# Decoder trunk on one core: the recurrence's gate products as 64-row products per head, with the input gates moved between partitions by DMA

## The chip, the cores and the metric

The kernel runs on one core of a Trainium2 chip, in one launch. The metric is the device time of one execution in microseconds (us). Engines are named as in the profile: PE (TensorE matmuls), PEld (its weight loads), DVE (VectorE), ACT (ScalarE), POOL (GpSimd) and SP (SyncE, which here only issues the weight DMAs).

## The reference

256 tokens of width 1024 go through two layers. Each has a token mixer, a channel mixer (dense in layer 0, top 2 of 8 experts in layer 1) and a gated embedding, all in f32. The change touches one part of the token mixer, the RG-LRU:

```python
ub = u.reshape(bsz, seq, 16, 64)                       # 16 heads of 64 channels
r      = sigmoid(einsum('bsnc,ncd->bsnd', ub, w_a) + b_a)
i_gate = sigmoid(einsum('bsnc,ncd->bsnd', ub, w_x) + b_x)
log_a = -8.0 * r * softplus(-lam)
a = exp(log_a)
b = sqrt(-expm1(2.0 * log_a)) * (i_gate * u)
h[s] = a[s] * h[s-1] + b[s]                            # scan over the tokens
y_a = h * gelu(rnn_gate)
```

Beside it stands a differential attention of 8 heads with rotary q and k: two 64-channel score products per head, two softmaxes, their difference times v. Both branches are projected, gated, added and projected again.

## The kernel before

**Tiling.** Activations lie transposed in SBUF, channels on the 128 partitions: a tile [128, 8, 256] holds 1024 channels (8 tile rows t) of 256 tokens, so that a tile row has two 64-channel heads, on partitions 0 to 63 and 64 to 127. Large weights come in chunks of 1 MB, in six raw slots. Each f32 weight w is split into two rounded parts, `whi` (ACT, helper `hi`, line 665) and `wlo` = w - whi (DVE, helper `lo`, line 1141), and a product takes three matmuls: whi by xhi, whi by xlo, wlo by xhi (line 1829). There are three slots for the split chunks.

**Steps.** The mixer is a loop over steps c = 0 to 35, written out on every engine in the same order: in step c PE multiplies chunk c (48 matmuls of 256 columns), then does the small products of that step. ACT and DVE in step c first split chunk c+3, ACT's halves waiting until PE has finished the halves of chunk c (`s_pe`), and then do their own work of step c. Nothing else orders the engines but semaphores; each engine's instructions run in the order in which they are written.

- Steps 0 to 3: DVE scales the chunk into `RIN` and convolves it to `U` (`convolve`, 8 instructions per step).
- Steps 2 to 5: PE multiplies two tile rows of `U` by the block-diagonal `BD` (`gate_products`, line 1984). Per tile row there are two f32 products of 128 rows: the one with `w_a` goes to the first half of a bank, the one with `w_x` to the second half. The matrix BD holds both heads of a tile row on its diagonal and zeros elsewhere. ACT makes `T2` = r, `IG` = i_gate, `TH` = tanh of a multiple of r, one instruction each (`gate_functions`, lines 786 to 790).
- Steps 4 to 11: ACT copies the q and k chunks to `QT`; POOL issues four DMAs per chunk that exchange 32-partition groups into `QW` (`exchange`, line 554); DVE rotates in steps 6 to 13 (`rotate`, three instructions).
- Step 6: DVE multiplies `IG` by `U` (line 1249), ahead of the split of chunk 9; ACT takes the square root of TH into `SQ`, which lies on `U`'s memory and therefore waits for that (line 832). Steps 7 and 8: ACT turns T2 into a = exp(...) (`decays`, line 797, four tile rows each). Steps 8 to 15: DVE makes one tile row of b per step (`recurrence_input`, lines 1258 and 1260). Steps 13 and 17: DVE scans four tile rows (`scan`, line 1266).
- Steps 14 to 25: the attention, one head per step on each engine. PE makes the `scores` of head c-14 (lines 1997 and 2000, products of 64 rows: the two halves of a head lie on partitions 0 to 63 and 64 to 127 and go to two banks), DVE masks and takes the maximum (line 1291 and 1294, result `AMX`), ACT takes the exponentials (lines 841 and 846), DVE the difference, PE turns it (line 2010), ACT copies it (`WT`, line 860), PE multiplies by v (line 2021). The first scores wait until all eight rotations are done.

`SPLAM`, needed by TH, comes from a chain of small DVE instructions in step 1 of layer 0 (`constants`).

## Time and profile before

| | |
|---|---|
| three runs, median (lowest to highest) | 1826.87 us (1825.75 to 1829.56) |
| the profiled execution: time, span | 1828.0 us, 1826.3 us |
| granted PE clock, mean | 0.994 |
| PE busy | 1784.4 us, 98% |
| PEld busy | 1563.4 us, 86% |
| DVE busy | 1490.7 us, 82% |
| ACT busy | 1307.7 us, 72% |
| POOL busy | 112.5 us, 6% |
| DMA | 517.04 MB, mean 283 GB/s |

The profiled execution is one, and lies 1.1 us above the median. Busy times are unions over the span. An f32 product appears as two matmul records. The mixer of layer 0 lies at about 20 to 227 us, that of layer 1 at about 546 to 750 us.

### The profile page before, as it was taken

The page shows a single profiled execution, that of the slowest core. Times are in us where ns is not written, and L with a number is a line of the kernel's source. Part 1 is how long each engine was busy: PE and PEld are TensorE (multiplying, and loading weights), DVE is VectorE, ACT ScalarE, POOL GpSimd, SP SyncE. Part 2 cuts the span into 40 slices and gives each one's busy share as a digit, 9 for nine tenths or more (in the row PEclk, how much of TensorE's full clock was granted, in tenths as well). Part 3 has the DMA queues.
Part 4 walks back from the last instruction along what each step waited for, and adds up shares of the span by engine and source line. Part 5 has one row for each costly group of instructions (what it writes and reads, how often), then busy time and mean ns, then how long its engine had stood idle before and what let it go on. Part 6 is the DMA issues. An engine that isn't in the chain of part 4 may idle for free.

```text
span 1826.3 us, 29866 instructions
## 1 busy us (share of the span) xinstructions
PE 1784.4 (98%) x10569; PEld 1563.4 (86%) x10569; DVE 1490.7 (82%) x1958; ACT 1307.7 (72%) x1732; POOL 112.5 (6%) x138
## 2 busy tenths in 40 slices
PE   6999999999999999999999999999999999999997
PEld 6998999999889999978888888888888888888786
DVE  7888667666478886769989989989899898998997
ACT  6756547454477657467888888788888887888787
POOL 1200000000010200012000000010000100000300
PEclk8999999999999999999999999999999999999999
DMA  9663555566556744667999999999999999999992
GB/s 307 206 191 117 174 200 191 185 198 205 188 158 193 221 141 139 208 185 258 395 382 379 387 363 392 374 369 389 365 383 374 374 389 372 375 384 363 391 363 95
DMA packets 276050, 517.04 MB, mean 283 GB/s; under 512 B 10754, under 2 KB 114052, under 8 KB 275972
## 3 DMA queue, kind: packets, MB, share of 16 engines
q1 hardware_dynamic: 268400, 493.81, 76.4%
q0 software_dynamic: 7248, 22.06, 3.7%
q8 instruction: 50, 0.82, 0.2%
q14 instruction: 28, 0.23, 0.0%
q10 hardware_dynamic: 324, 0.12, 0.0%
HBM read 503.87 MB, written 7.88 MB: 280 GB/s over the span
## 4 chain that ended last, share of the span: by engine, by line
PE 78%; DVE 9%; ACT 8%; issue 2%; DMA 2%; ACTq 0%; DVEq 0%; SPq 0%
PE bank L1829 74%; DVE wlo L1141 4%; ACT whi L665 2%; DMA raw<-in_moe_w_up_dram 1%; PE bank L2299 1%; ACT SC L846 1%; ACT SQJ L676 1%; PE bank L1984 1%; DVE RIN L1266 1%; DVE SC L1294 1%; ACT L1052 0%; ACT L665 0%; ACT SC L841 0%; ACT L772 0%; ACT HH L728 0%
## 5 line engine op out<-in xcount | busy, mean ns | idle before, releaser
L1141 DVE TENSOR_TENSOR wlo<-raw,whi 128x1024 fp32r<-128x1024 f32 x880 | 1031.0, 1222 | 164.3 <-ACT whi L665 161.6
L665 ACT ACTIVATE whi<-raw 128x1024 fp32r<-128x1024 f32 x880 | 917.1, 1059 | 306.3 <-PE bank L1829 288.2
L1829 PE MATMUL bank<-HH,whi 128*128 128x256 f32 x1296 | 364.1, 281 | 0.0
L1829 PE MATMUL bank<-whi,XGH 128*128 128x512 f32 x896 | 355.8, 397 | 5.7 <-DVE wlo L1141 5.6
L1829 PE MATMUL bank<-HL,whi 128*128 128x256 f32 x1296 | 360.1, 278 | 0.0
L1829 PE MATMUL bank<-HH,wlo 128*128 128x256 f32 x1296 | 360.1, 278 | 0.0
L1829 PE MATMUL bank<-whi,XGL 128*128 128x512 f32 x896 | 350.5, 391 | 0.0
L1829 PE MATMUL bank<-wlo,XGH 128*128 128x512 f32 x896 | 349.4, 390 | 0.0
L1829 PEld LDWEIGHTS bank<-HH,wlo 128*128 128x128 f32 x1296 | 244.5, 189 | 0.0
L1829 PEld LDWEIGHTS bank<-HH,whi 128*128 128x128 f32 x1296 | 243.6, 188 | 0.9 <-issue 0.7
L1829 PEld LDWEIGHTS bank<-HL,whi 128*128 128x128 f32 x1296 | 243.8, 188 | 0.2
L1829 PEld LDWEIGHTS bank<-whi,XGH 128*128 128x128 f32 x896 | 168.6, 188 | 44.8 <-DVE wlo L1141 10.9
L1829 PEld LDWEIGHTS bank<-whi,XGL 128*128 128x128 f32 x896 | 168.4, 188 | 36.5
L1829 PEld LDWEIGHTS bank<-wlo,XGH 128*128 128x128 f32 x896 | 168.7, 188 | 33.2
L1829 PE MATMUL bank<-whi,ATH 128*128 128x512 f32 x448 | 176.8, 395 | 0.0
L1829 PE MATMUL bank<-whi,ATL 128*128 128x512 f32 x448 | 175.0, 391 | 0.0
L1829 PE MATMUL bank<-wlo,ATH 128*128 128x512 f32 x448 | 174.4, 389 | 0.0
L1829 PEld LDWEIGHTS bank<-whi,ATL 128*128 128x128 f32 x448 | 84.1, 188 | 18.1
L1829 PEld LDWEIGHTS bank<-wlo,ATH 128*128 128x128 f32 x448 | 84.2, 188 | 16.9
L1829 PEld LDWEIGHTS bank<-whi,ATH 128*128 128x128 f32 x448 | 84.1, 188 | 16.8
L1526 DVE TENSOR_TENSOR wlo<-raw,whi 128x1024 fp32r<-128x1024 f32 x56 | 67.2, 1223 | 31.1 <-ACT whi L951 29.9
L951 ACT ACTIVATE whi<-raw 128x1024 fp32r<-128x1024 f32 x56 | 58.8, 1059 | 42.1 <-PE bank L1829 41.4
(359 smaller groups left out, 2098.9 us busy)
## 6 DMA issues: line engine op xcount, KB each, us to landing
raw<-in_moe_w_gate_dram SPq DMA_DIRECT2D x112, 1024.0 KB, 8.0
raw<-in_moe_w_up_dram SPq DMA_DIRECT2D x112, 1024.0 KB, 8.6
raw<-in_moe_w_down_dram SPq DMA_DIRECT2D x112, 1024.0 KB, 7.2
raw<-in_w_in_dram SPq DMA_DIRECT2D x56, 1024.0 KB, 6.0
raw<-in_ffn_w_gate_dram SPq DMA_DIRECT2D x14, 1024.0 KB, 5.1
raw<-in_ffn_w_up_dram SPq DMA_DIRECT2D x14, 1024.0 KB, 5.1
raw<-in_ffn_w_down_dram SPq DMA_DIRECT2D x14, 1024.0 KB, 5.0
raw<-in_w_proj_a_dram SPq DMA_DIRECT2D x8, 1024.0 KB, 5.1
```

The source lines that it names most:

```text
L665: nc.scalar.activation(whi[b % SPL][:, r], raw[b % RAW][:, r], ACT.Copy).then_inc(s_hi, 1)
L676: nc.scalar.activation(SQJ[:, 0:src.shape[-1]], src, ACT.Square, accum_out=sums).then_inc(s, 1)
L846: ins = nc.scalar.activation(r, r, ACT.Exp, bias=AMX[:, q, 2 + m:3 + m], scale=HD ** -0.5, accum_out=ASUM[:, q, 2 + m:3 + m])
L951: nc.scalar.activation(whi[nb % SPL][:, r], raw[nb % RAW][:, r], ACT.Copy).then_inc(s_hi, 1)
L1141: v.tensor_tensor(wlo[b % SPL][:, r], raw[b % RAW][:, r], whi[b % SPL][:, r].bitcast(F32), ALU.subtract).then_inc(s_lo, 1)
L1266: ins = v.tensor_tensor_scan(RIN[:, i, 3:], T2[:, i, :], IG[:, i, :], 0.0, ALU.mult, ALU.add)
L1294: ins = v.tensor_tensor_reduce(SC[:, q, SEQ * (m + 1):SEQ * (m + 2)], B[4 + m][:, P:P + SEQ], MASK[:, :], 1.0, -3e38, ALU.add, ALU.max, AM ...
L1526: v.tensor_tensor(wlo[nb % SPL][:, r], raw[nb % RAW][:, r], whi[nb % SPL][:, r].bitcast(F32), ALU.subtract).then_inc(s_lo, 1)
L1829: ins = mm(dst, a, b, start=start and n == 0, stop=stop and n == 2, skip_group_check=True)
L1984: ins = mm(bank[:, SEQ * kind:SEQ * kind + SEQ], BD[:, kind, t, :], U[:, t, :], start=True, stop=True)
L2299: ins = nc.tensor.transpose(B[6][:, P * i:P * i + P], MA[:, f % 2, P * i:P * i + P], IDENT[:, :])
```

## The change

`BD` becomes one matrix per tile row. Its rows 0 to 63 hold, side by side, w_a and w_x of the lower head, its rows 64 to 127 w_x and w_a of the upper head, and no zeros are left. Each tile row still has two f32 products, but each now uses 64 rows: the lower head's result (r on partitions 0 to 63, i on 64 to 127) goes to one bank and then to `T2`, the upper head's (i on 0 to 63, r on 64 to 127) to another bank and then to `IG`. Since i comes out on the other head's partitions, POOL moves it: per pair of tile rows two DMAs of 64 partitions write `IX`, which lies on `V`'s memory. TH and the decays read r from two tiles and so take two instructions of 64 partitions each. `SQ` now lies on `K` (in place of TH) instead of on `U`. DVE multiplies IX by U in step 8 instead of step 6, and makes two tile rows of b per step in steps 8 to 11 instead of one per step in steps 8 to 15. New waits: the decays and the multiplication on the DMAs (`s_ix`), the copy of V in step 12 and the rotations of k on b (`s_bl`), the second product on a bank's earlier reader (`s_tc`, layer 0). The bias rows b_a and b_x are loaded twice each in halves, so that they fit the partitions; b_x by two DMAs of POOL ahead of its first memsets. POOL's two memsets of BD are gone.

```diff
-        BD = at("BD", o_bd, [P, 2, KT, P])
+        BD = at("BD", o_bd, [P, KT, P])
-        SQ = at("SQ", o_gel, [P, KT, SEQ])
+        IX = at("IX", o_q + 16 * KB, [P, KT, SEQ])
-        OALL, TH = Q, K
+        OALL, TH, SQ = Q, K, K
+        LRU_BANK = ((3, 7), (5, 6))
...
@@ gpsimd
+            v = lru_bx.rearrange("l (t p) -> (l t) p", p=P)
+            for h in range(2):
+                pool.dma_start(R2[96 + 16 * h:112 + 16 * h, HD - HD * h:P - HD * h],
+                               v[:, HD * h:HD * h + HD]).then_inc(s_ldp, 16)
...
-            pool.memset(BD[:, :, :, :], 0.0).then_inc(s_bdz, 1)
...
-                        pool.dma_start(BD[HD * h:HD * h + HD, kind, :, HD * h:HD * h + HD], pairs[h]).then_inc(s_bd, 16)
+                        d = HD * (kind ^ h)
+                        pool.dma_start(BD[HD * h:HD * h + HD, :, d:d + HD], pairs[h]).then_inc(s_bd, 16)
...
+            def input_halves(layer, j):
+                pool.wait_ge(s_gx, 4 * layer + j + 1)
+                two = slice(2 * j, 2 * j + 2)
+                pool.dma_start(IX[0:HD, two, :], T2[HD:P, two, :]).then_inc(s_ix, 16)
+                pool.dma_start(IX[HD:P, two, :], IG[0:HD, two, :]).then_inc(s_ix, 16)
...
             def exchange(layer):
+                input_halves(layer, 0)
+                input_halves(layer, 1)
                 for i in range(8):
                     n = 8 * layer + i
+                    if i in (1, 2):
+                        input_halves(layer, i + 1)
                     pool.wait_ge(s_eva, eva(layer, 4 + i))
...
@@ scalar
-                    bank = B[3 if t % 2 == 0 else 7]
                     col = layer * KT + t
-                    link(nc.scalar.activation(T2[:, t, :], bank[:, 0:SEQ], ACT.Sigmoid, bias=V2[:, 80 + col:81 + col]))
-                    nc.scalar.activation(IG[:, t, :], bank[:, SEQ:], ACT.Sigmoid, bias=V2[:, 96 + col:97 + col])
+                    for h, dst in enumerate((T2, IG)):
+                        c = 96 + 16 * h + col
+                        ins = nc.scalar.activation(dst[:, t, :], B[LRU_BANK[t % 2][h]][:, 0:SEQ], ACT.Sigmoid,
+                                                   bias=V2[:, c:c + 1])
+                    link(ins)
+                    if t % 2:
+                        act.sem_inc(s_gx, 1)
...
-                    nc.scalar.activation(TH[:, t, :], T2[:, t, :], ACT.Tanh,
-                                         scale=SPLAM[:, col:col + 1]).then_inc(s_ga, 1)
+                    for h, src in enumerate((T2, IG)):
+                        r = slice(HD * h, HD * h + HD)
+                        ins = nc.scalar.activation(TH[r, t, :], src[r, t, :], ACT.Tanh, scale=SPLAM[r, col:col + 1])
+                    ins.then_inc(s_ga, 1)
...
             def decays(layer, g):
+                act.wait_ge(s_ix, 128 * (layer + 1))
...
-                    ins = nc.scalar.activation(T2[:, t, :], T2[:, t, :], ACT.Exp, scale=SPNEG[:, col:col + 1])
+                    for h, src in enumerate((T2, IG)):
+                        r = slice(HD * h, HD * h + HD)
+                        ins = nc.scalar.activation(T2[r, t, :], src[r, t, :], ACT.Exp, scale=SPNEG[r, col:col + 1])
...
                         if c == 12:
                             act.wait_ge(s_rc, 6 * layer + 2)
+                            act.wait_ge(s_bl, KT * layer + KT)
...
                     if c == 6:
                         act.wait_ge(s_ga, KT * (layer + 1))
-                        act.wait_ge(s_iu, layer + 1)
...
@@ vector
             def input_gates(layer):
-                dve.wait_ge(s_ga, KT * (layer + 1))
-                v.tensor_tensor(IG[:, :, :], IG[:, :, :], U[:, :, :], ALU.mult).then_inc(s_iu, 1)
+                dve.wait_ge(s_ix, 128 * (layer + 1))
+                v.tensor_tensor(IX[:, :, :], IX[:, :, :], U[:, :, :], ALU.mult).then_inc(s_iu, 1)
...
                 dve.wait_ge(s_qs[i % 4], 64 * (2 * layer + i // 4 + 1))
+                if i >= 4:
+                    dve.wait_ge(s_bl, KT * layer + 2 * i - 6)
...
-                    if c == 6:
-                        input_gates(layer)
...
-                    if 8 <= c < 16:
-                        recurrence_input(layer, c - 8)
+                    if c == 8:
+                        input_gates(layer)
+                    if 8 <= c < 12:
+                        recurrence_input(layer, 2 * c - 16)
+                        recurrence_input(layer, 2 * c - 15)
...
@@ tensor
+                if n == 1:
+                    pe.wait_ge(s_tc, 4)
-                for kind in range(2):
-                    ins = mm(bank[:, SEQ * kind:SEQ * kind + SEQ], BD[:, kind, t, :], U[:, t, :],
-                             start=True, stop=True)
+                for h in range(2):
+                    r = slice(HD * h, HD * h + HD)
+                    ins = mm(B[LRU_BANK[t % 2][h]][:, 0:SEQ], BD[r, t, :], U[r, t, :], start=True, stop=True)
```

DVE, steps 7 (its last two rows here) and 8, before:

```order
L1282 TENSOR_TENSOR Q<-QT,COSR 128x512
L1283 TENSOR_TENSOR Q<-Q,QW 128x512 [waits s_dc]
L1141 TENSOR_TENSOR wlo_60<-raw_54,whi_57 128x1024 [waits s_hi] x2
L1281 TENSOR_TENSOR QW<-QW,SINR 128x512 [waits s_qs2]
L1282 TENSOR_TENSOR Q<-QT,COSR 128x512
L1283 TENSOR_TENSOR Q<-Q,QW 128x512 [waits s_dc]
L1258 SCALAR_TENSOR_TENSOR SQ<-T_96,SQ 128x256 [waits s_al,s_iu,s_sq]
L1260 TENSOR_TENSOR IG<-IG,SQ 128x256 [waits s_dc]
```

and step 8 with the head of step 9 now (`K` is the memory that SQ lies on):

```order
L1169 TENSOR_TENSOR wlo_60<-raw_54,whi_57 128x1024 [waits s_hi] x2
L1311 TENSOR_TENSOR QW<-QW,SINR 128x512 [waits s_qs2]
L1312 TENSOR_TENSOR Q<-QT,COSR 128x512
L1313 TENSOR_TENSOR Q<-Q,QW 128x512 [waits s_dc]
L1277 TENSOR_TENSOR IX<-IX,U 128x2048 [waits s_ix]
L1286 SCALAR_TENSOR_TENSOR K<-T_96,K 128x256 [waits s_al,s_iu,s_sq]
L1288 TENSOR_TENSOR IG<-IX,K 128x256 [waits s_dc]
L1286 SCALAR_TENSOR_TENSOR K<-T_96,K 128x256
L1288 TENSOR_TENSOR IG<-IX,K 128x256 [waits s_dc]
L1169 TENSOR_TENSOR wlo_58<-raw_49,whi_55 128x1024 [waits s_hi] x2
```

The multiplication of 2048 elements per partition has moved behind the rotation of step 8, and a second tile row of b stands behind it, ahead of the split of step 9.

ACT, steps 7 and 8 before (L797 are the decays, L665 the split of chunk 11):

```order
L797 ACT_TABLE_LOAD
L797 ACTIVATE T_96<-T_96,SM 128x256 x4
L665 ACTIVATE whi_57<-raw_54 128x1024 [waits s_pe,s_w5]
L665 ACTIVATE whi_57<-raw_54 128x1024 [waits s_pe]
L812 ACTIVATE QT<-bank 128x512 [waits s_qr]
L797 ACTIVATE T_96<-T_96,SM 128x256 x4
```

and step 7's now:

```order
L825 ACT_TABLE_LOAD
L825 ACTIVATE T_96<-T_96,SM 64x256 [waits s_ix]
L825 ACTIVATE T_96<-IG,SM 64x256
L825 ACTIVATE T_96<-T_96,SM 64x256
L825 ACTIVATE T_96<-IG,SM 64x256
L825 ACTIVATE T_96<-T_96,SM 64x256
L825 ACTIVATE T_96<-IG,SM 64x256
L825 ACTIVATE T_96<-T_96,SM 64x256
L825 ACTIVATE T_96<-IG,SM 64x256
L684 ACTIVATE whi_57<-raw_54 128x1024 [waits s_pe,s_w5]
```

Four instructions of 128 partitions have become eight of 64, ahead of the split for which DVE's step 8 waits.

POOL, the exchanges of steps 5 and 6 now (before, the QW rows stood alone, one after another):

```order
L554 DMA IX<-T_96 64x512 [waits s_gx]
L555 DMA IX<-IG 64x512
L572 DMA QW<-QT 32x512 [waits s_u,s_eva]
L572 DMA QW<-QT 32x512 x3
L554 DMA IX<-T_96 64x512 [waits s_gx]
L555 DMA IX<-IG 64x512
L572 DMA QW<-QT 32x512 [waits s_u,s_eva]
L572 DMA QW<-QT 32x512 x3
```

The last two IX DMAs stand between the second and the third exchange.

## Rows read from the trace of the kernel before

**Rows 1.** The page, part 1: busy us, share of the span, instructions.
```profile
PE 1784.4 (98%) x10569; PEld 1563.4 (86%) x10569; DVE 1490.7 (82%) x1958; ACT 1307.7 (72%) x1732; POOL 112.5 (6%) x138
```

**Rows 2.** Chain of waits, layer 0, 63 to 119 us: start, length, what.
```profile
63.37 45.24 PE bank L1829 x384
108.63 1.07 ACT whi L665
...
113.59 2.44 DVE RIN L1266 x4
116.05 2.36 DVE wlo L1141 x2
```

**Rows 3.** The same chain in layer 1.
```profile
563.51 1.99 PE bank L1984 x8
...
587.47 45.24 PE bank L1829 x384
...
640.15 2.36 DVE wlo L1141 x2
```

**Rows 4.** Timeline of PE, attention: start, length, line, operands, [idle before, releaser].
```profile
177.44 0.52 PE L2010 MATMUL bank<-IDENT,SC 128*128 128x128 f32 x3 [1.05 <-ACT WT L860]
...
701.54 0.52 PE L2010 MATMUL bank<-IDENT,SC 128*128 128x128 f32 x3 [1.05 <-ACT WT L860]
```

**Rows 5.** Timeline of PE, layer 0, the gate products of step 2.
```profile
38.99 1.89 PE L1984 MATMUL bank<-U,BD 128*128 128x256 f32 x8
40.52 0.47 PE L1829 MATMUL bank<-HH,whi 128*128 128x256 f32 x1
40.83 0.28 PE L1829 MATMUL bank<-HL,whi 128*128 128x256 f32 x1
```

**Rows 6.** Timeline of PE, layer 0, the first scores, products of 64 rows.
```profile
113.97 0.28 PE L1829 MATMUL bank<-whi,HL 128*128 128x256 f32 x1
114.17 0.49 PE L1997 MATMUL bank<-K,Q 64*128 64x128 f32 x4
114.50 0.60 PE L2000 MATMUL bank<-K,Q 64*128 64x256 f32 x4
115.03 0.39 PE L1829 MATMUL bank<-whi,HH 128*128 128x256 f32 x1
115.25 0.28 PE L1829 MATMUL bank<-wlo,HH 128*128 128x256 f32 x1
```

**Rows 7.** Chain of waits, layer 0, step 3.
```profile
45.83 0.51 ACT K L790
...
47.66 1.13 PE bank L1984 x4
```

**Rows 8.** Timeline of ACT, layer 0, steps 7 and 8.
```profile
77.57 1.71 ACT L797 ACTIVATE T<-T,SM 128x256 f32<-128x256 f32 x4
79.19 2.24 ACT L665 ACTIVATE whi<-raw 128x1024 fp32r<-128x1024 f32 x2
```

**Rows 9.** Timeline of DVE, layer 0, steps 6, 8 and 9.
```profile
65.78 2.29 DVE L1249 TENSOR_TENSOR IG<-IG,U 128x2048 f32<-128x2048 f32 x1 [1.64 <-ACT K L790]
...
80.26 2.42 DVE L1141 TENSOR_TENSOR wlo<-raw,whi 128x1024 fp32r<-128x1024 f32 x2 [1.16 <-ACT whi L665]
82.60 0.68 DVE L1281 TENSOR_TENSOR QW<-QW,SINR 128x512 f32<-128x512 f32 x1
...
84.53 0.42 DVE L1258 SCALAR_TENSOR_TENSOR SQ<-T,SQ 128x256 f32<-128x256 f32 x1
...
85.33 1.22 DVE L1141 TENSOR_TENSOR wlo<-raw,whi 128x1024 fp32r<-128x1024 f32 x1
87.11 1.22 DVE L1141 TENSOR_TENSOR wlo<-raw,whi 128x1024 fp32r<-128x1024 f32 x1 [0.57 <-ACT whi L665]
```

**Rows 10.** POOL's timeline, one exchange; DMA issues, KB each and us to landing.
```profile
63.51 1.96 POOL L554 DMA_DIRECT2D QW<-QT  x4 [2.04 <-ACT QT L812]
...
QW<-QT POOLq DMA_DIRECT2D x64, 64.0 KB, 4.5
```

More of the change, by code:

```diff
@@ L281, in bass_hybrid_rglru_diffattn_moe @@
         s_iu = sem("s_iu")
+        s_gx = sem("s_gx")
+        s_ix = sem("s_ix")
         s_bl = sem("s_bl")
@@ L1229, in convolve @@
                 if j == 0:
-                    dve.wait_ge(s_bdz if layer else s_pool, 3 if layer else 12)
+                    dve.wait_ge(s_bdz if layer else s_pool, 1 if layer else 12)
                 for tap in range(4):
@@ L1981, in gate_products @@
                     pe.wait_ge(s_ga, n - 1)
-                bank = B[3 if t % 2 == 0 else 7]
-                for kind in range(2):
-                    ins = mm(bank[:, SEQ * kind:SEQ * kind + SEQ], BD[:, kind, t, :], U[:, t, :],
-                             start=True, stop=True)
+                if n == 1:
+                    pe.wait_ge(s_tc, 4)
+                for h in range(2):
+                    r = slice(HD * h, HD * h + HD)
+                    ins = mm(B[LRU_BANK[t % 2][h]][:, 0:SEQ], BD[r, t, :], U[r, t, :], start=True, stop=True)
                 ins.then_inc(s_gt, 1)
```

12 lines of the change are left out of this document (6 added, 6 removed).

## The prediction

> **What bounds the kernel now.** I read the page first: PE is busy 98% of the span [rows 1], so any PE time saved looks like time saved. Then the chain of waits in order of time, because a share of 98% is an average. In layer 0 the chain runs on PE for 45.24 us, steps 6 to 13, and then leaves it: at 108.63 it is ACT's split that has waited for PE, then DVE up to the scan at 113.59 and the next split at 116.05 [rows 2]. From there it goes back and forth between DVE (split, mask, maximum) and ACT (exponentials, copy of WT, split), and returns to PE at 177.44, where PE had stood idle 1.05 us for ACT's WT. Layer 1 has the same picture: PE from 587.47, the split at 640.15, PE idle 1.05 us at 701.54 [rows 3, 4]. So in each layer the attention is a loop of DVE and ACT that starts when DVE is through with step 13's scan, and PE's end of the attention is that start plus a constant. The question for every edit is: what does it do to the moment at which DVE starts the split of step 14 (116.05, 640.15)? Call it the start of the loop. What PE saves before it counts only if that moment comes earlier.
>
> **The gate products.** Before, a group of two tile rows costs, from 38.99 to the second matmul behind it at 40.83, 1.84 us, less the 0.12 that a chunk's matmul takes anyway (45.24 / 384): 1.72, or 0.43 for each of four f32 products [rows 5]. What two 64-row products on the two halves cost is shown by the scores: a pair of 128 columns and a pair of 256 take 115.25 - 113.97 - 2 x 0.12 = 1.04 us, and by columns two single products would be 0.21 + 0.43 = 0.64 [rows 6]. So the two of a pair run together, and 0.40 goes at the two ends of the group. The new group is two pairs of 256: 2 x 0.43 + 0.40 = 1.26. It saves 0.46, eight times. Bounds: no saving and the 0.40 on top (the products one after another), or 0.86 (no cost at the ends).
>
> The Trainium skill says this too (TensorEngine Tiling, Theoretical Speedup and Key Properties): up to a factor of 2 where the contraction is 64 or less, but a change of tiling mode drains TensorE; it gives no price for the drain. By the factor alone a group would cost 0.86, and the sum below would come out near 0 instead of +2.6. The scores' rows show the 0.40 that the drain rule lets one expect, so I go by the rows.
>
> **ACT in steps 2 to 5.** Each tile row gets one more activation (TH in two). The trace has none of 64 partitions on ACT. Four of 128 take 79.19 - 77.57 = 1.62, or 0.40 each [rows 8]. Either a half costs as much as a whole, since it has the same 256 columns, or half, 0.20. I take 0.40: the scores' 64-row products show no saving by rows either. In step 3 of layer 0 this is on the path: ACT waits for SPLAM until 45.83, and PE's second half of the group (47.66) waits for TH of tile row 1 [rows 7]. Two more activations put that at 48.46, and then 0.43 + 0.20 instead of 0.86: 0.57 later than before, which also swallows the saving of step 2. Steps 4 and 5 save 0.92. So PE reaches step 6 of layer 0 only 0.35 early. In layer 1 nothing waits there except for U at step 2, before the group starts (563.51) [rows 3], so PE is 4 x 0.46 = 1.84 early. The chain does not pass through ACT in steps 4 and 5 of layer 0 or in steps 2 to 5 of layer 1, so I cost the other extra activations, 0.8 per step, at nothing; if ACT's idle time there did not hold them, each 0.1 over would be 0.1 later in step 6.
>
> **ACT in step 7.** Eight decays of 64 partitions instead of four stand ahead of the split (79.19) for which DVE's step 8 waits (80.26, idle 1.16 for ACT's whi) [rows 8, 9]. ACT works without a pause from its square root to there. At 0.40 each this is +1.6 us, in both layers. In step 8 another 1.6, which step 9's idle time on ACT takes. The square root loses its wait for `s_iu`, but that was over at 65.78 + 2.29 = 68.07 [rows 9], and from the start of step 7's decays back through two table loads, the square root and the split ACT came to it later: nothing.
>
> **DVE in steps 8 to 13.** Before, DVE goes from 80.26 to 116.05, 35.79 us, and in each of steps 9 to 13 it stands idle 0.57 for ACT's split, thus for PE [rows 9]. After, it has six splits of 2.3, six rotations of 1.93 (84.53 - 82.60), the multiplication 2.3 (now here instead of in step 6, where DVE idled for ACT anyway), eight tile rows of b at 0.80 (85.33 - 84.53) instead of six, and the scan 2.46 (116.05 - 113.59): 13.8 + 11.6 + 2.3 + 6.4 + 2.5 = 36.6. That is more than 35.8, so DVE no longer waits for anyone and the start of the loop comes 0.8 later, counted from a start of step 8 that is itself 1.6 later. Together +2.4 per layer against PE's position. The two tile rows of b taken out of steps 14 and 15 give nothing back: DVE idled behind them for ACT.
>
> What lies behind DVE: the eighth rotation ends some 2 us later relative to PE, and PE's first scores wait for it. Chunk splits come up to 4 us later than now, but PE needs chunk 12's only at 63.37 + 6 x 5.65 = 97.3, and DVE has it at 81.9 + 8.1 + 2.3 = 92.3. The copy of V in step 12 now waits for the last b, 81.9 + 8.1 + 3 x 5.8 = 107.4; its bank is wanted by PE at 115.03 [rows 6]. QT copies 6 and 7 slip by some 1.5 us, waiting for rotations; an exchange is 2.0 of issue and 4.5 of landing [rows 10], and rotation 6 comes two steps behind its copy: over 3 us are left.
>
> **POOL and the DMAs.** Eight IX DMAs per layer at 0.49 of issue (1.96 / 4) [rows 10]. The last pair is released by the last IG of step 5, before ACT's last tanh ends, which was at 65.78, now 0.8 later [rows 9], and is issued by 67.6; 64 KB land in 4.5 us [rows 10], 128 KB by twice that at most, 76.6. The decays want them at 77.57: nothing, as long as this 1 us of cover stands; beyond it each microsecond costs one. At the start POOL's two DMAs come ahead of its memsets and the 8 KB memset of BD goes: the transposes of x that wait for POOL are not on the path there, nothing either way, 0.3 at most.
>
> **Sum.** Layer 0: 2.4 - 0.35 = +2.0. Layer 1: 2.4 - 1.84 = +0.6. Together +2.6 us. Behind the attention PE is the bound in both layers and passes a shift on whole. Against the profiled execution's 1828.0 this is 1830.6; that execution lies 1.1 above the median of the three runs, so against 1826.87 it is 1829.5.
>
> **Rivals.**
> 1. *The loop's start stays tied to PE* (faster). If DVE caught up before step 13, only step 13's tile row of b would be gone from the path, 0.8 per layer, and PE's leads would count: -1.6 - 0.35 - 1.84 = -3.8, 1823.1. For it: DVE had idle time. Against: five times 0.57 is 2.85, and what is added is 2.3 + 1.6 + 1.6.
> 2. *The 64-row products do not run together* (slower). A group costs 4 x 0.43 + 0.40 = 2.12, each 0.40 more than now. Layer 0 comes 1.0 later at step 3 and 0.8 over steps 4 and 5, layer 1 1.6 later: 4.8 + 1.8 + 1.6 = +8.2, 1835.1. It decides from the point where a pair takes more than 0.65. For it: U as the moving operand comes fresh, and tile rows alternate between banks. Against: the scores' pairs.
> 3. *Half activations cost more than 0.40* (slower): two 64-partition instructions that read different tiles and write one may not follow each other as closely. At 0.50 the decays take 4.0 instead of 1.6, +0.8 more per layer: +4.2, 1831.1.
> 4. *Half activations cost 0.20*: then ACT adds nothing, layer 0 keeps its 1.84 too, and 1.6 - 3.7 = -2.1 is left, 1824.8. With the skill's factor taken alone it is 1826.9. Both are no change, as the forecast is.
>
> **How the numbers follow.** What a measurement of this kernel can tell from no change is about 0.2%, 3.65 us: 1823.2 to 1830.5. The forecast with its variants under 4 (all within that band): 0.56. Rival 1: 0.13, faster. Rival 2: 0.09, and rival 3: 0.22, both slower, 0.31 together; rival 3 has so much because the forecast stands only 1 us below the band's edge and the dearer case needs little. The range goes from just above rival 1 to above rival 3, 1823.5 to 1832.0; outside are most of rival 1 and rival 2.
>
> **What the profile after would show.** Gate groups of 1.2 to 1.3 us from first product to the chunk behind them; the group of step 3 in layer 0 waiting for TH as late as 48.4. Four tile rows of decays in 3.2 us. On DVE no idle time for ACT's whi from step 9 to step 13, and the scan starting about 115.6 in layer 0. PE idle 1.5 to 2 us before the first scores of each layer, released by DVE's K: a wait that was not there. The chain leaving PE at step 7 or so instead of step 13, through ACT's decays and DVE. The prediction would be wrong if DVE still idled in steps 12 and 13 (rival 1), if a gate group took 2.1 (rival 2), or if the decays waited for the IX DMAs.

## The result

The changed kernel takes 1833.16 us, median of 8 runs (1831.36 to 1834.29); the kernel before, beside it on the same chip, 1826.79 us (1825.48 to 1829.87, 8 runs). The ratio is 1.0031, 95% interval 1.0022 to 1.0040: 6.4 us slower by the medians, 4 to 7 by the interval. The forecast was 1829.5 with a range of 1823.5 to 1832.0, no change that can be measured. The direction of the sum was right (+2.6), its size was not, and the likeliest case was the wrong one.

The profiled execution took 1834.3 us, its span is 1832.4 us, 6.1 us longer than before's. One execution of e5_dve_alone below, 2229.41 us at a mean granted clock of 0.75 against 0.993 to 0.997 in its others, is in the slow state and is left out of its ratio; without it that kernel's median is 1828.56 instead of 1828.73.

### The profile page after: what moved, and what is told of

Read it like the earlier page. It is cut to its first block, busy times and chain, and to the rows that moved or that the text cites. A ratio compares the mean times of both kernels' runs of the same rounds, so it can differ in the third digit from the quotient of the medians.

```text
span 1832.4 us, 29932 instructions
## 1 busy us (share of the span) xinstructions
PE 1783.6 (97%) x10569; PEld 1561.4 (85%) x10569; DVE 1489.2 (81%) x1958; ACT 1326.5 (72%) x1764; POOL 116.0 (6%) x154
## 4 chain that ended last, share of the span: by engine, by line
PE 53%; DVE 5%; ACT 5%; issue 2%; DMA 1%; ACTq 0%; DVEq 0%
PE bank L1860 50%; DVE wlo L1169 3%; ACT whi L684 1%; PE bank L2332 1%; DMA raw<-in_moe_w_up_dram 1%; ACT L1080 0%; ACT L684 0%; PE bank L2342 0%; ACT SC L874 0%; ACT SQJ L695 0%; PE bank L2274 0%; ACT L791 0%; ACT Y L1087 0%; DVE RIN L1294 0%; DVE SC L1324 0%
## 5 line engine op out<-in xcount | busy, mean ns | idle before, releaser
L1169 DVE TENSOR_TENSOR wlo<-raw,whi 128x1024 fp32r<-128x1024 f32 x880 | 1028.9, 1221 | 175.1 <-ACT whi L684 172.1
L684 ACT ACTIVATE whi<-raw 128x1024 fp32r<-128x1024 f32 x880 | 917.2, 1059 | 265.9 <-PE bank L1860 250.6
L1860 PE MATMUL bank<-HH,whi 128*128 128x256 f32 x1296 | 363.6, 281 | 0.0
L1860 PE MATMUL bank<-whi,XGH 128*128 128x512 f32 x896 | 355.4, 397 | 5.7 <-DVE wlo L1169 5.7
L1860 PE MATMUL bank<-HL,whi 128*128 128x256 f32 x1296 | 360.3, 278 | 0.0
L1860 PE MATMUL bank<-HH,wlo 128*128 128x256 f32 x1296 | 360.2, 278 | 0.0
L1860 PE MATMUL bank<-whi,XGL 128*128 128x512 f32 x896 | 350.2, 391 | 0.0
L1860 PE MATMUL bank<-wlo,XGH 128*128 128x512 f32 x896 | 349.3, 390 | 0.0
L1860 PEld LDWEIGHTS bank<-HH,whi 128*128 128x128 f32 x1296 | 244.1, 188 | 3.3 <-issue 3.3
L1860 PEld LDWEIGHTS bank<-HH,wlo 128*128 128x128 f32 x1296 | 245.1, 189 | 0.0
L1860 PEld LDWEIGHTS bank<-HL,whi 128*128 128x128 f32 x1296 | 244.5, 189 | 0.0
L1860 PEld LDWEIGHTS bank<-whi,XGH 128*128 128x128 f32 x896 | 168.5, 188 | 44.0 <-DVE wlo L1169 10.1
L1860 PEld LDWEIGHTS bank<-whi,XGL 128*128 128x128 f32 x896 | 168.4, 188 | 36.2
L1860 PEld LDWEIGHTS bank<-wlo,XGH 128*128 128x128 f32 x896 | 168.7, 188 | 33.2
L1860 PE MATMUL bank<-whi,ATH 128*128 128x512 f32 x448 | 176.8, 395 | 0.0
L1860 PE MATMUL bank<-whi,ATL 128*128 128x512 f32 x448 | 175.0, 391 | 0.0
L1860 PE MATMUL bank<-wlo,ATH 128*128 128x512 f32 x448 | 174.4, 389 | 0.0
L1860 PEld LDWEIGHTS bank<-whi,ATL 128*128 128x128 f32 x448 | 84.1, 188 | 18.0
L1860 PEld LDWEIGHTS bank<-wlo,ATH 128*128 128x128 f32 x448 | 84.2, 188 | 16.9
L1860 PEld LDWEIGHTS bank<-whi,ATH 128*128 128x128 f32 x448 | 84.1, 188 | 16.8
```

Of the source, the lines that this page charges most:

```text
L684: nc.scalar.activation(whi[b % SPL][:, r], raw[b % RAW][:, r], ACT.Copy).then_inc(s_hi, 1)
L1169: v.tensor_tensor(wlo[b % SPL][:, r], raw[b % RAW][:, r], whi[b % SPL][:, r].bitcast(F32), ALU.subtract).then_inc(s_lo, 1)
L1860: ins = mm(dst, a, b, start=start and n == 0, stop=stop and n == 2, skip_group_check=True)
```

## The profile after

The page's first part, which answers to [rows 1]:

```profile
PE 1783.6 (97%) x10569; PEld 1561.4 (85%) x10569; DVE 1489.2 (81%) x1958; ACT 1326.5 (72%) x1764; POOL 116.0 (6%) x154
```

PE's busy time is 0.8 us less than before, although the kernel is 6 us longer: PE's time without work grows from 41.9 to 48.8 us. ACT has 32 instructions and 18.8 us more.

Line numbers have moved: L1829 is now L1860, the splits L665 and L1141 are L684 and L1169, the decays L797 are L825, the gate products L1984 are L2018.

Names used below: the *start of the loop* is the start of DVE's split of step 14, as in the prediction; the *table load* is ACT's `ACT_TABLE_LOAD` ahead of step 7's decays; *PE's long run* are the 504 matmuls in a row behind the attention; a *half* is an activation of 64 partitions.

PE, layer 0: the second pair of products of step 3 (answers to [rows 7]), the gate group of step 4 and what surrounds it (to [rows 5]), and the first scores (to [rows 6]), with the idle time ahead in brackets:

```profile
49.65 0.70 PE L2018 MATMUL bank<-U,BD 64*128 64x256 f32 x4 [1.21 <-ACT K L815]
...
55.92 0.28 PE L1860 MATMUL bank<-HH,wlo 128*128 128x256 f32 x1
56.13 1.14 PE L2018 MATMUL bank<-U,BD 64*128 64x256 f32 x8
57.20 0.39 PE L1860 MATMUL bank<-HH,whi 128*128 128x256 f32 x1
57.42 0.28 PE L1860 MATMUL bank<-HL,whi 128*128 128x256 f32 x1
...
117.74 0.72 PE L2030 MATMUL bank<-K,Q 64*128 64x128 f32 x4 [2.69 <-DVE K L1313]
```

From the last matmul of the chunk at 55.92 to the second behind the group at 57.42 there are 1.50 us, of which two matmuls of a chunk would take 0.24: the group costs 1.26, exactly as forecast. Step 3's second pair comes at 49.65 (47.66 before, 48.46 forecast). And PE stands idle 2.69 us before the first scores.

ACT in step 3 of layer 0, where it waits for SPLAM and makes TH of two tile rows (answers to [rows 7]):

```profile
46.56 0.51 ACT L815 ACTIVATE K<-T,SPLAM 64x256 f32<-64x256 f32 x1 [2.71 <-DVE SPLAM L1376]
47.09 0.50 ACT L815 ACTIVATE K<-IG,SPLAM 64x256 f32<-64x256 f32 x1
...
48.57 0.51 ACT L815 ACTIVATE K<-T,SPLAM 64x256 f32<-64x256 f32 x1
49.09 0.50 ACT L815 ACTIVATE K<-IG,SPLAM 64x256 f32<-64x256 f32 x1
```

From the first TH to PE's second pair there are 49.65 - 46.56 = 3.09 us, before 47.66 - 45.83 = 1.83: 1.26 more, where the forecast had 0.80.

ACT, step 7 of layer 0 (answers to [rows 8]):

```profile
77.09 1.28 ACT L825 ACT_TABLE_LOAD   x1
78.38 0.51 ACT L825 ACTIVATE T<-T,SM 64x256 f32<-64x256 f32 x1
78.91 0.51 ACT L825 ACTIVATE T<-IG,SM 64x256 f32<-64x256 f32 x1
...
82.03 0.50 ACT L825 ACTIVATE T<-IG,SM 64x256 f32<-64x256 f32 x1
82.56 2.01 ACT L684 ACTIVATE whi<-raw 128x1024 fp32r<-128x1024 f32 x2
```

The eight decays take 82.56 - 78.38 = 4.18 us, 0.52 each. Before, four took 1.62. The forecast had 3.2.

DVE, layer 0, from step 8 to the start of the loop (answers to [rows 9] and [rows 2]):

```profile
83.65 2.36 DVE L1169 TENSOR_TENSOR wlo<-raw,whi 128x1024 fp32r<-128x1024 f32 x2 [3.73 <-ACT whi L684]
...
87.86 2.29 DVE L1277 TENSOR_TENSOR IX<-IX,U 128x2048 f32<-128x2048 f32 x1
...
117.61 2.43 DVE L1294 TENSOR_TENSOR_SCAN RIN<-T,IG 128x256 f32<-128x256 f32 x4
120.07 1.23 DVE L1169 TENSOR_TENSOR wlo<-raw,whi 128x1024 fp32r<-128x1024 f32 x1
```

Behind 83.65 no row up to the start of the loop has an idle time in brackets: DVE waits for nobody. Its run is 120.07 - 83.65 = 36.42 us (forecast 36.6, before 35.79). In layer 1 the same: split of step 8 at 608.75, start of the loop at 645.18 (before 640.15).

TensorE's granted clock (PEclk, 1.00 is 2.4 GHz, 0.50 is 1.2), four stretches of 4 us of layer 1's attention; stretch, PE busy (instructions), PEclk, DMA share, GB/s. Before:

```profile
643.00:647.00 4.00, 4.00 (x35) 1.00 0.82 262
708.00:712.00 4.00, 4.00 (x36) 1.00 0.42 147
```

after:

```profile
643.00:647.00 4.00, 4.00 (x23) 0.57 0.62 217
708.00:712.00 4.00, 4.00 (x24) 0.57 0.15 30
```

and the chain of waits where it returns to PE in layer 1, before:

```profile
703.30 5.76 PE bank L1829 x48
710.39 5.57 PE bank L1829 x48
...
730.35 65.47 PE bank L1829 x504
```

after:

```profile
708.34 7.29 PE bank L1860 x48
716.96 5.57 PE bank L1860 x48
...
736.92 65.47 PE bank L1860 x504
```

Forty-eight matmuls that took 5.76 us take 7.29. From the start of the loop to PE's long run there are 730.35 - 640.15 = 90.20 us before and 736.92 - 645.18 = 91.74 after. That was in no part of the forecast. All of it arises at 708: from the loop's start to these 48 matmuls there are 63.15 us before (703.30 - 640.15) and 63.16 after (708.34 - 645.18), so the half clock behind the first scores at 643 cost nothing in this profile. From 648 to 708 PEclk is 1.00 in every stretch of 4 us, and just ahead of the 48 matmuls PE is idle 1.24 us for ACT's WT, 1.05 before [rows 4]:

```profile
706.58 0.52 PE L2043 MATMUL bank<-IDENT,SC 128*128 128x128 f32 x3 [1.24 <-ACT WT L888]
```

**The ledger of the two profiles.** Every line is a difference of two times in the traces (after less before).

| piece | forecast | measured | from |
|---|---|---|---|
| start to the table load of layer 0 | -0.35 | +0.82 | 77.09 - 76.27; of it SPLAM's arrival 46.56 - 45.83 = +0.73 |
| table load to DVE's split of step 8, both layers | +3.2 | +5.13 | (83.65 - 77.09) - (80.26 - 76.27) = 2.57; layer 1: 2.56 |
| DVE's run, both layers | +1.6 | +1.27 | 36.42 - 35.79 = 0.63; layer 1: 0.64 |
| loop start of layer 0 to table load of layer 1 | -1.84 | -2.19 | (602.20 - 120.07) - (600.37 - 116.05) |
| loop start of layer 1 to PE's long run | 0 | +1.54 | 91.74 - 90.20 |
| from there to the end | 0 | -0.47 | (1832.4 - 736.92) - (1826.3 - 730.35) |
| sum | +2.6 | +6.1 | |

Two theories for the excess. A: the decays' spacing, 0.52 instead of 0.40, is the larger part, and the rest is the granted clock, which falls where PE has waited. B: the order of DVE's work (the multiplication and the early tile rows of b) or the 64-row products cost more than their rows show.

## The experiments

All ratios are against runs of the kernel before on the same chip, with 95% intervals. The changed kernel's 1833.16 us is from the first series; e1 to e4 were timed in another, so a difference of totals between them mixes two series, and the spans between rows of the profiles are the firmer measure.

### e1_grouped

```diff
-                for t in range(4 * g, 4 * g + 4):
-                    col = layer * KT + t
-                    for h, src in enumerate((T2, IG)):
-                        r = slice(HD * h, HD * h + HD)
+                for h, src in enumerate((T2, IG)):
+                    r = slice(HD * h, HD * h + HD)
+                    for t in range(4 * g, 4 * g + 4):
+                        col = layer * KT + t
```

> The changed kernel, with the eight 64-partition decays of a step in another order: the four on partitions 0 to 63 first, then the four on 64 to 127. In the changed kernel's trace they alternate and start 0.52 us apart, against 0.40 for whole ones before. Theory A (the 0.12 is the price of changing the partitions or the tile read from one instruction to the next): 0.40 apart but for one, the split of step 7 starts 0.85 us earlier per layer, the whole is 1.7 us faster than the changed kernel. Theory B (every activation of 64 partitions costs 0.52): nothing changes, 0.0 us. Theory C (each waits for the one before it because they write one tile): nothing changes either, and whole ones that write one tile would then cost it too, which they don't.

1830.15 us, 1.0018 (1.0010 to 1.0027): 3.0 us less than the changed kernel, 1.7 expected; the two intervals overlap. ACT, step 7 of layer 0:

```profile
77.51 1.71 ACT L825 ACTIVATE T<-T,SM 64x256 f32<-64x256 f32 x4
79.23 1.70 ACT L825 ACTIVATE T<-IG,SM 64x256 f32<-64x256 f32 x4
80.96 2.01 ACT L684 ACTIVATE whi<-raw 128x1024 fp32r<-128x1024 f32 x2
```

Eight in 80.96 - 77.51 = 3.45 us. Four in a row busy ACT for 1.71 us, just as four whole ones did [rows 8]: a half costs what a whole costs, and some 0.12 more goes where the partitions change: once in the middle, and once more ahead of the split of 128 partitions, which the expectation did not count. Theory A holds; B and C of the expectation fall. The split of step 8 comes 5.83 us after the start of the table load, against 6.56: 0.73 per layer instead of the expected 0.85. In layer 1 there is no half clock at 643 or 708 either, and from the loop's start to PE's long run there are 90.42 us instead of 91.74, which is where the total gains more than expected.

### e2_whole_decays

```diff
-                    for h, src in enumerate((T2, IG)):
-                        r = slice(HD * h, HD * h + HD)
-                        ins = nc.scalar.activation(T2[r, t, :], src[r, t, :], ACT.Exp, scale=SPNEG[r, col:col + 1])
+                    ins = nc.scalar.activation(T2[:, t, :], T2[:, t, :], ACT.Exp, scale=SPNEG[:, col:col + 1])
```

> The changed kernel with four whole decays per step instead of eight halves; it leaves out reading r of the upper heads from its own tile (it takes i in its place). Theory (ACT's 2.56 us in step 7 pass to the start of the attention loop one for one, since DVE no longer waits for anyone from step 9 on): loop starts 2.56 us earlier in each layer, total 5.1 us faster than the changed kernel, so 1 us slower than before. Rival (DVE's start of step 8 is covered otherwise, or the 64-row products and the clock at the start are the cause): 1 us or less.

1826.16 us, 0.9997 (0.9989 to 1.0006): 7.0 us less than the changed kernel, level with before. So everything in the change but the decays' halves comes to -0.4 us (-2.0 to +1.1), where the forecast's other terms come to 2.6 - 3.2 = -0.6. From the table load to the start of the loop there are 40.43 and 40.47 us, 42.98 in both layers of the changed kernel: the decays' 2.5 us per layer pass to the loop whole. The two loops start at 117.18 and 639.70. Beyond the 5.1 expected it gained 1.9 us; with PE's shorter wait the half clock at 643 and 708 is gone too (not that in layer 0, at 116), and from loop to long run there are 729.90 - 639.70 = 90.20 us.

### e3_mult_early

```diff
                 for c in range(MIX - 4):
+                    if c == 8:
+                        input_gates(layer)
                     if c < 35:
                         lo(b + c + SPL)
...
-                    if c == 8:
-                        input_gates(layer)
```

> The changed kernel with DVE's multiplication IX by U at the head of step 8, ahead of the split instead of behind the rotation. DVE idles 3.73 us there for ACT's split, and the DMAs have landed. Theory: its 2.3 us fall into that idle time, the loop starts 2.3 us earlier in each layer, 4.6 us faster than the changed kernel, about 1.8 us slower than before. Rival (the split of step 8 must come out by a time set by PE or the rotations): less than 1 us.

1829.06 us, 1.0015 (1.0006 to 1.0024): 4.1 us less than the changed kernel, 4.6 expected. The loop starts at 117.56 and 640.99, 34.8 us after the split of step 8 instead of 36.4. That is 1.6 us per layer, not the 2.3 of the expectation; the total comes near it because the half clock at 643 and 708 is gone here too (90.19 us from loop to long run). Where the other 0.7 went stands in DVE's step 9:

```profile
89.31 2.36 DVE L1169 TENSOR_TENSOR wlo<-raw,whi 128x1024 fp32r<-128x1024 f32 x2 [0.67 <-ACT whi L684]
```

ACT's decays of step 8 are longer by 2.5 us as well, and with the multiplication out of the way DVE waits for the split behind them. The multiplication was on the path, as forecast, for its place only.

### e4_before_halves

```diff
-                    ins = nc.scalar.activation(T2[:, t, :], T2[:, t, :], ACT.Exp, scale=SPNEG[:, col:col + 1])
+                    for h in range(2):
+                        r = slice(HD * h, HD * h + HD)
+                        ins = nc.scalar.activation(T2[r, t, :], T2[r, t, :], ACT.Exp, scale=SPNEG[r, col:col + 1])
```

> The kernel before with nothing but each decay split into two activations of 64 partitions (same tile read and written). Theory: a step of decays takes 8 x 0.52 = 4.2 us instead of 1.6, DVE's step 8 starts 2.56 us later, but DVE idles 5 x 0.57 = 2.85 us in steps 9 to 13 and catches up: the loop starts within 0.5 us of before, total 0 to 1 us slower. Rival (what ACT loses in step 7 is never caught up): 5.1 us slower, which is the whole of the loss. If a half that reads and writes the same tile costs 0.40, the decays take 3.2 us, and the 0.12 belongs to the change of tile.

1828.78 us, 1.0012 (1.0003 to 1.0020). ACT in step 7, then DVE in steps 8 and 9:

```profile
77.64 4.15 ACT L799 ACTIVATE T<-T,SM 64x256 f32<-64x256 f32 x8
81.81 2.02 ACT L665 ACTIVATE whi<-raw 128x1024 fp32r<-128x1024 f32 x2
```

```profile
82.91 2.36 DVE L1143 TENSOR_TENSOR wlo<-raw,whi 128x1024 fp32r<-128x1024 f32 x2 [3.73 <-ACT whi L665]
...
89.45 2.36 DVE L1143 TENSOR_TENSOR wlo<-raw,whi 128x1024 fp32r<-128x1024 f32 x2 [1.46 <-ACT whi L665]
```

Alternating halves of one and the same tile cost 0.52 too, so it is the change of partitions and not of the tile. The same +2.56 us on ACT, with DVE's slack still there, shifts the loop by only 0.8 us per layer (116.90 - 76.35 = 40.55 from the table load to the loop, 39.78 before). Even so this is more than the expected 0.5 per layer and 0 to 1 in all: the total is 2.2 us slower (0.5 to 3.7). ACT loses 2.5 us a second time, in step 8, and DVE waits for it again at 89.45. In the changed kernel DVE had no slack left and all of it passed on.

### e5_dve_alone

```diff
-        SQ = at("SQ", o_gel, [P, KT, SEQ])
...
-        OALL, TH = Q, K
+        OALL, TH, SQ = Q, K, K
...
-                        act.wait_ge(s_iu, layer + 1)
...
+                if i >= 4:
+                    dve.wait_ge(s_bl, KT * layer + 2 * i - 6)
...
-                    if c == 6:
-                        input_gates(layer)
...
-                    if 8 <= c < 16:
-                        recurrence_input(layer, c - 8)
+                    if c == 8:
+                        input_gates(layer)
+                    if 8 <= c < 12:
+                        recurrence_input(layer, 2 * c - 16)
+                        recurrence_input(layer, 2 * c - 15)
```

> The kernel before with DVE's part of the change alone: SQ on K, the multiplication IG by U at step 8 behind the rotation, two tile rows of b per step from 8 to 11, rotations of k waiting for b. Gates, activations and DMAs as before. Theory: DVE's run from the split of step 8 to the start of the loop is 36.4 us as in the changed kernel, against 35.8 before, without idle time from step 9 on; the loop starts 0.65 us later in each layer, total 1.3 us slower than before. Rival 1 of the prediction (the loop's start is tied to PE and DVE catches up): 0.8 us earlier per layer, 1.6 us faster.

1828.73 us, 1.0011 (1.0002 to 1.0021), which holds the expected +1.3 but not -1.6. From the table load to the loop: 118.16 - 77.67 = 40.49 and, in layer 1, 643.22 - 602.71 = 40.51, against 39.78: +0.72 per layer. Rival 1 is out, and so is theory B for DVE's part.

### e6_filler, e7_after_again

e7_after_again is the changed kernel unchanged; the filler:

```diff
                 if h == 0:
+                    for i in range(20):
+                        mm(B[4][:, 0:SEQ], HH[:, 0, 0:P], HH[:, i % KT, :], start=True, stop=True)
                     pe.wait_ge(s_qr, 8 * layer + 8)
```

> The changed kernel with 20 matmuls of 128x256 on PE ahead of the first scores of each layer, whose result nobody reads; at 0.113 us each they last 2.3 us and fit into the 2.69 us for which PE waits there. In the changed kernel's trace the granted clock stood at half from 117.7 to 121.1, from 643.3 to 646.7 and from 708.2 to 711.6 us, none of it in the trace of before. Theory (the wait is what lets the clock fall, and the lost PE time ends up in the total): no half clock at 117.7 and 643.3, 1 to 2 us faster than the changed kernel. Rival (at these places PE has slack, and the fall at 708 has nothing to do with the wait): clock stays up at 117.7 and 643.3, total unchanged, 0 +/- 0.7 us.

> The changed kernel once more, for a second profile. Theory (loop start 4.0 us later in layer 0 and 5.0 in layer 1, which come back in every execution; the half clock at the start of the kernel does not): 6.4 us slower than before, loop starts within 1 us of 120.1 and 645.2, gaps of DVE the same. If the half clock at 117.7, 643.3 and 708.2 is there again, it belongs to the kernel; if only the first two are, the third was chance and part of the profile's 6.1 us with it.

e7 (4 runs): 1833.70 us, 1.0042 (1.0027 to 1.0057). Loops at 119.95 and 644.83, the half clock again at all three places, and 91.78 us from loop to long run. PE's idle time ahead of the first scores is 2.70 us in layer 0, but 4.36 in layer 1 (2.69 in the first profile). The cause of that difference is PE's pace: at a granted clock of 1.00 in both, the matmuls of a chunk follow one another 0.118 us apart in one profile and 0.113 in the other, and over the 384 of steps 6 to 13 that is 1.7 us. What sets the pace is open.

e6 (6 runs): 1831.78 us, 1.0033 (1.0021 to 1.0045), PEclk in e6:

```profile
643.00:647.00 4.00, 4.00 (x35) 1.00 0.44 154
708.00:712.00 4.00, 4.00 (x36) 1.00 0.28 60
```

The clock stays up, and from the start of the loop (644.56) to PE's long run (734.78) there are 90.22 us, as in before. The filler takes PE's idle time before layer 1's first scores down to 0.33 us. But the two intervals of the totals overlap; the totals alone settle nothing. And ahead of 708 PE's wait for WT is 1.05 us here, 1.24 in e7, so the filler kernel differs from the changed one at both places.

### e10_filler_l1, e11_after_third

In e10 the range of the loop is `20 * layer`, so only layer 1 has the filler; e11 is the changed kernel again.

> The changed kernel with the 20 unread matmuls ahead of the first scores in layer 1 only. In both profiles of the changed kernel the clock stood at half from 117.6, 643.3 and 708.1 us, and with the filler in both layers in none of these; from the start of the loop in layer 1 to the end the filler kernel took 1185.1 us and the changed one 1187.0 and 1187.2. Theory (the fall in layer 1 costs 2 us, the one in layer 0 nothing, because PE waits for the loop there): the fall at 117.6 is there, those at 643 and 708 are not, and the time is that of the filler in both layers, about 1.8 us below the changed kernel. Rival (the loss is elsewhere, or the filler's own matmuls cost what they save): 0.5 us or less below the changed kernel.

> The changed kernel on the same chip as the two others of this call, so that the filler's gain has a comparison of its own. Theory: 6.4 to 7 us slower than before, the half clock at 117.6, 643.3 and 708.1 again, 1187 us from the start of the loop in layer 1 to the end.

e10: 1834.04 us (5 runs), 1.0036 (1.0022 to 1.0049). e11: 1831.73 us (7 runs), 1.0033 (1.0021 to 1.0044). A miss in the totals: the filler's kernel isn't faster. Its profile has a fall of the clock at 50 us that no other has, and reaches step 7 of layer 0 2.3 us later than e11's; that accounts for the profiled execution, not for the four others. The local claim holds: the fall at 117 is there, and there is no half clock in layer 1's attention, with 90.01 us from the loop's start to PE's long run. In e11, after waits of 4.36 us in both layers, the clock was at half around 117 and 643 (PEclk 0.50 over 643 to 647) and not at 708; there it is 90.92, and the 0.7 us are lost before 709.05 (63.87 us behind the loop's start, 63.15 before). Put together, that stretch is 90.0 to 90.4 us in each profile without half clock in it (before, e1 to e6, e10 and the two below), 91.7 and 91.8 in the two with the fall at 708, 90.9 in e11.

What makes the clock fall at 708 is not shown. The two profiles that have it have both a fall at 643 and a wait of 1.24 us for WT. e1 and e5 have the wait of 1.24 without a fall at 643, and no fall follows:

```profile
704.22 0.52 PE L2043 MATMUL bank<-IDENT,SC 128*128 128x128 f32 x3 [1.24 <-ACT WT L888]
```

e11 has the fall at 643 with a wait of 1.05, and none follows there either. Between the two places lie 60 us at full clock, so the tie to PE's new wait rests on these few profiles.

### c8_spread

Left out of the diff: `s_ix` becomes two semaphores, and the waits that go with it.

```diff
...
-                for t in range(4 * g, 4 * g + 4):
+                for h, src in enumerate((T2, IG)):
+                    r = slice(HD * h, HD * h + HD)
+                    for t in (2 * g, 2 * g + 1):
...
-                    if c in (7, 8):
+                    if 7 <= c < 11:
                         decays(layer, c - 7)
...
-            def input_gates(layer):
-                dve.wait_ge(s_ix, 128 * (layer + 1))
-                v.tensor_tensor(IX[:, :, :], IX[:, :, :], U[:, :, :], ALU.mult).then_inc(s_iu, 1)
+            def input_gates(layer, g):
+                dve.wait_ge(s_ix[g], 64 * (layer + 1))
+                r = slice(4 * g, 4 * g + 4)
+                v.tensor_tensor(IX[:, r, :], IX[:, r, :], U[:, r, :], ALU.mult).then_inc(s_iu, 1)
...
+                    if c in (6, 8):
+                        input_gates(layer, (c - 6) // 2)
                     if c < 35:
                         lo(b + c + SPL)
```

> The changed kernel with the decays in four groups of two tile rows, one per step in steps 7 to 10, the halves on partitions 0 to 63 ahead of those on 64 to 127; and the multiplication IX by U in two halves of four tile rows, at the head of step 6 (where DVE idles 4.1 us) and at the head of step 8 (3.7 us). Theory: ACT is back at the pace of before at step 8 (split about 80.3), 1.15 us of multiplication are hidden in each place, DVE catches up with PE by step 13 and the loop starts one tile row of b (0.8 us) earlier than before in layer 0 and 2.6 us earlier in layer 1: 3 us faster than before, 9.5 us faster than the changed kernel. Rival (the multiplication at the head of step 6 delays the split of chunk 9, which PE or ACT wants at once; or the first scores' wait for the last rotation holds): no faster than before.

1822.91 us, 0.9979 (0.9970 to 0.9988): 3.4 us faster than before, 10.8 us faster than the changed kernel in the same series (e7). DVE:

```profile
64.77 1.22 DVE L1279 TENSOR_TENSOR IX<-IX,U 128x1024 f32<-128x1024 f32 x1
68.98 2.58 DVE L1170 TENSOR_TENSOR wlo<-raw,whi 128x1024 fp32r<-128x1024 f32 x2 [2.99 <-ACT whi L684]
...
79.20 1.22 DVE L1279 TENSOR_TENSOR IX<-IX,U 128x1024 f32<-128x1024 f32 x1
80.65 2.36 DVE L1170 TENSOR_TENSOR wlo<-raw,whi 128x1024 fp32r<-128x1024 f32 x2 [0.23 <-ACT whi L684]
```

Both halves of the multiplication lie in DVE's idle time, the split of step 8 is back at 80.65, and the loops start at 114.70 and 635.54 (116.05 and 640.15 before): 1.35 and 4.61 us earlier, where 0.8 and 2.6 were expected, although the total is about as expected. PE no longer waits for the first scores. In layer 1 ACT now waits 0.39 us for the last IX DMA ahead of the table load at 596.92, a wait that the changed kernel doesn't have.

### e9_before_spread

Left out of the diff: SQ on K and the rotations' wait, as in e5, and the waits for the four groups of decays.

```diff
...
-                for t in range(4 * g, 4 * g + 4):
+                for t in (2 * g, 2 * g + 1):
                     col = layer * KT + t
                     ins = nc.scalar.activation(T2[:, t, :], T2[:, t, :], ACT.Exp, scale=SPNEG[:, col:col + 1])
...
-                    if c in (7, 8):
+                    if 7 <= c < 11:
...
-                    if 8 <= c < 16:
-                        recurrence_input(layer, c - 8)
+                    if 8 <= c < 12:
+                        recurrence_input(layer, 2 * c - 16)
+                        recurrence_input(layer, 2 * c - 15)
```

> The kernel before with c8_spread's order of work but the gates of before: SQ on K, the decays whole, in four groups of two tile rows in steps 7 to 10, two tile rows of b per step from 8 to 11, the multiplication left in step 6. It asks how much of c8_spread's 3.4 us is the order and how much the 64-row products. Theory (ledger of the traces: 64-row gates give 2.9 us over both layers, the order 0.8 us per layer because step 13's tile row of b goes): 1.6 us faster than before, loop starts 0.8 us earlier in each layer. Rival (the order alone does it, ACT's shorter step 7 lets DVE in earlier by 0.8 us more per layer): 3.2 us faster, and the 64-row products are worth nothing.

1825.41 us, 0.9994 (0.9985 to 1.0003). The loops start at 115.24 (0.81 earlier) and 638.52 (1.63 earlier over both layers), as the theory has it; the total (1.0 us faster by the medians) can't be told from before. Of the 1.35 and 4.61 us by which c8's loops are earlier than before's, the order of work alone gives 0.81 and 1.63. From layer 0's loop to layer 1's table load the kernels with the old gates take 484.3 to 484.6 us (before, e4, e5, e9) and all those with the 64-row products 481.9 to 482.9: the 64-row products do give some 2.2 us in layer 1.

## Why the prediction was wrong

In short: the decays in halves were priced at 0.40 each and cost 0.52, because they alternate between the partition halves. That alone would have made the sum 2.6 + 1.9, or 1831.4 us, still inside the range. What carried the time past 1832.0 are two more: half clock of PE in layer 1's attention, 1.5 us, which the sum did not have and which only profiles with PE's new wait show, and the same 0.52 at a second place, step 3.

**What bounds the kernel: right.** The loop's start sets PE's end of the attention: 90.2 us lie between them in layer 1, in kernels whose loops start between 635.5 and 647.2.

**The gate products: right in price, a little low in yield.** 1.26 per group to the hundredth; layer 1's share of the way came 2.2 us shorter instead of 1.84. Rival 2 is out. The Trainium skill (TensorEngine Tiling (Array Packing), Theoretical Speedup) gives up to a factor of 2 where a dimension is 64 or less; the trace agrees with it as an upper bound, 1.72 became 1.26 and not 0.86.

**ACT in step 7: this is the step that failed.** "At 0.40 each this is +1.6 us, in both layers." The term was +3.2 and measured +5.13. That a half costs as much as a whole was right, e1 shows it; but the change had the halves alternate, and then one follows the other 0.52 us later. Shown by e1 (grouped, 0.40 but for the changes), e4 (same tile, alternating, 0.52) and e2 (whole: level with before). The same text put the 1.6 us of step 8's decays at nothing, since "step 9's idle time on ACT takes" them; that held only while DVE was late itself. Where it isn't (e3, e4), DVE's step 9 waits 0.67 and 1.46 us for them. Rival 3 had the place and about the size (0.50), with the wrong reason: it blamed the two tiles. It was given 0.22 and was the case that came true; its own sum, 1831.1, fell short by the clock and by step 3, below.

**DVE in steps 8 to 13: right.** 36.42 against 36.6, no idle time behind step 8, +0.72 per layer alone in e5. That the slack of 2.85 us would be used up was the premise by which ACT's loss counts in full; e4 shows what it would have cost with the slack left, 0.8 instead of 2.56. What the change didn't use: DVE's idle time ahead of step 8 grew from 1.16 to 3.73 us, and the multiplication that stands behind the rotation would have fitted there (e3).

**What lies behind DVE: its consequence was missed.** The idle time of PE before the first scores was forecast ("1.5 to 2 us", measured 2.69 to 4.36) and costed at nothing. After it the granted clock was at half in all three profiles of the changed kernel. With PE kept at work through the wait it didn't fall (both layers of e6, layer 1 of e10). The fall right behind the wait in layer 1 cost nothing in two profiles and 0.7 us in the third; the later one at 708 cost 1.5 us in the first two. Only profiles with a fall at 643 show the one at 708, but that the wait causes it was not shown.

**Step 3 and the start of the kernel: the first term failed by the same price.** Forecast -0.35 at step 7, measured +0.82. From SPLAM's arrival to PE's second pair the change costs 1.26 us in every profile that has the new gates (3.08 or 3.09 instead of 1.83), where the prediction took two activations more at 0.40, 0.80: TH's halves alternate too. With these 0.46 the term is +0.1, and the table load does come 30.53 us after SPLAM's arrival, 30.44 before. The other 0.73 is that arrival itself, 46.56 instead of 45.83, and it differs from execution to execution (45.90 to 46.72 with the new gates), with the clock at the start: from 12 to 26 us PEclk is 0.51 in this execution, 0.63 in before's and 1.00 in others. At a low clock there (0.51 and 0.52) the changed kernel has its table load at 77.09 and 76.95, and e5, with the old gates and also at 0.51, at 77.67. In that one profile SPLAM comes at 46.97 and PE's products of step 3 don't wait for it, so a start at low clock may hide the cost; one profile doesn't show it.

**POOL and the DMAs: right.** ACT's decays and DVE's multiplication follow the instruction before them without a wait; a median landing of 5.6 and 6.3 us and a last issue at 68.00 (layer 1: 593.15) end ahead of the table loads at 77.09 and 602.20.

**What stays open.** The pieces that come back in every profile of the changed kernel, without SPLAM's arrival and the end, make 0.1 + 5.1 + 1.3 - 2.2 = +4.3 us, and with what the clock costs in layer 1's attention 5.0 to 5.9. The medians say 6.4, 7.4 and 5.3 in three series. Whether the rest, 0.3 to 1.5 us, is the clock at the start, or the stretch behind PE's long run, which differs by up to 1.7 us between profiles of the changed kernel, was not settled. The totals of the filler kernels (1.9 us below the changed kernel in one series, 2.3 above it in the other) don't confirm what the clock is worth.

## What to carry over

When an instruction is cut into pieces by partitions, cost each piece like the whole, order the pieces so that those on the same partitions follow one another, and look for every place where such pieces stand on the path (here the decays and TH). Before an engine's slack is spent twice (here DVE's, on its own new work and on ACT's delay), add up both; with the same work spread over the steps that have idle time, the change was worth 3.4 us instead of costing 6.4, some of it by the new order alone. A wait that costs PE nothing by the chain may still be followed by matmuls at half clock.

## What the runs showed of the hardware

- ACT, 256 f32 columns per partition: 0.40 us from one to the next, for 128 partitions and for 64 alike; 0.52 where 64-partition activations alternate between partitions 0 to 63 and 64 to 127, on one tile or two (TH and the decays of the changed kernel, e4), and again ahead of an activation of 128 partitions (e1).
- PE stood idle 2.69 us ahead of 117.74 and 642.85 in the changed kernel, and the matmuls right behind ran at 1.2 GHz (PEclk 0.50 from 118 to 120 us). At 708, with 1.24 us of idle time ahead, 48 matmuls took 7.29 us at PEclk 0.57 instead of 5.76; in e1 and e5 the same idle time was not followed by half clock. An idle time of 1.97 us in layer 1 of e1 was not followed by half clock, one of 1.77 in layer 0 of e2 was (PEclk 0.63 from 116 to 118).
- At a granted clock of 1.00 the f32 matmuls of 256 columns followed one another 0.118 us apart in some stretches and 0.113 in others, also in the same stretch of two executions of one kernel: PE's idle time ahead of layer 1's first scores was 2.69 us in one and 4.36 in the other.
- The first chunk at the start ran at 1.2 GHz in some executions and at 2.4 in others of the same kernel (PEclk 0.51 and 1.00 from 12 to 26 us in two profiles of the changed one). Of the 74 runs of before beside the experiments, 31 have a mean granted clock of 0.997 or more and a median of 1825.9 us, 37 have 0.994 or less and 1826.7.
